# A hybrid decoder step: the chunked mixers' tiles overlapped, and the sample tile's state products on 64 rows, two heads side by side

## What is computed

```python
def _mlstm(...):            # A, by chunks, the carried state is (C, n, m)
    s = einsum('bthd,bjhd->btjh', qc, kc) * exp(d_log - m_t)
    num = einsum('btjh,bjhd->bthd', s, vc) + w_inter * einsum('bthk,bhkv->bthv', qc, C)
    den = sum(s, axis=2) + w_inter * einsum('bthk,bhk->bth', qc, n)
    h = num / maximum(abs(den), exp(-m_t))
    C_new = carry_w * C + einsum('bjh,bjhk,bjhv->bhkv', w_j, kc, vc)
def _retention(...):        # B, the carried state is R
    s = einsum('bthd,bjhd->btjh', qc, kc) * d_mask
    o = einsum('btjh,bjhv->bthv', s, vc) + xi * einsum('bthk,bhkv->bthv', qc, R)
    R_new = g_chunk * R + einsum('jh,bjhk,bjhv->bhkv', zeta, kc, vc)
def _rwkv7(...):            # D, one step per token on S
    s_kk = einsum('bhvk,bhk->bhv', S, kk_t)
    S = S * w_t - s_kk * (kk_t * a_t) + v_t * k_t
    o_t = einsum('bhvk,bhk->bhv', S, r_t)
```

## Time and profile before

| | |
|---|---|
| median of three timed runs | 2622.53 us (2621.73 to 2622.9) |
| the profiled execution | 2619.64 us |
| its span, first to last instruction | 2617.4 us |
| mean granted clock of TensorE | 0.956 |

### The profile page before, as it was taken

How to read it: one execution, slowest core, us unless ns; L and a number is a source line. 1 busy time by engine, 2 the same in 40 slices (tenths; PEclk the granted TensorE clock), 3 DMA queues, 4 the chain that set the end, 5 groups by cost and what they waited for, 6 DMA issues and landing times. The chain is left out here.

```text
span 2617.4 us, 31827 instructions
## 1 busy us (share of the span) xinstructions
PE 2467.3 (94%) x13578; PEld 1809.7 (69%) x13578; DVE 813.1 (31%) x1619; ACT 465.1 (18%) x983; POOL 110.6 (4%) x208
## 2 busy tenths in 40 slices
PE   7989998888999999999989899988799999999997
PEld 6867674463784788888877667654548748888886
DVE  4242233534032644000132422434340336430012
ACT  2332122001130222100023321120111312220000
POOL 0011100000000000000001111000000000000000
PEclk9999988969999999999999999889699999999999
DMA  7101002222442222222131011022233432222220
GB/s 259 65 33 35 33 1 86 67 85 99 161 157 101 81 97 72 89 65 65 65 115 65 33 34 34 33 90 61 84 123 121 164 121 72 77 84 65 83 78 35
DMA packets 137675, 215.07 MB, mean 82 GB/s; under 512 B 35528, under 2 KB 69632, under 8 KB 137408
## 3 DMA queue, kind: packets, MB, share of 16 engines
q1 hardware_dynamic: 135232, 208.84, 23.5%
q10 hardware_dynamic: 2304, 4.20, 0.4%
HBM read 198.43 MB, written 14.58 MB: 81 GB/s over the span
## 5 line engine op out<-in xcount | busy, mean ns | idle before, releaser
L2118 PE MATMUL psum<-big,ring 128*128 128x288 f32 (+1 forms) x2048 | 471.2, 393 | 0.0
L2118 PEld LDWEIGHTS psum<-big,ring 128*128 128x128 f32 x2048 | 388.5, 190 | 79.9 <-DMA ring<-in_w_down 0.4
L580 PE MATMUL psum<-xT,ring 128*128 128x256 f32 (+1 forms) x1536 | 360.6, 397 | 8.6 <-DMA ring<-in_w_in 6.0
L580 PEld LDWEIGHTS psum<-xT,ring 128*128 128x128 f32 x1536 | 294.0, 192 | 70.8 <-DMA ring<-in_w_in 6.3
L627 PE MATMUL psum<-xT,ring 128*128 128x256 f32 (+1 forms) x768 | 227.1, 423 | 0.2
L2061 PE MATMUL psum<-tmp 128*128 128x272 f32 x768 | 181.4, 393 | 0.0
L2061 PEld LDWEIGHTS psum<-tmp 128*128 128x128 f32 x768 | 145.8, 190 | 30.8 <-issue 0.8
L627 PEld LDWEIGHTS psum<-xT,ring 128*128 128x128 f32 x768 | 136.8, 195 | 43.0 <-issue 15.3
L331 DVE SCALAR_TENSOR_TENSOR xtok<-xtok,psum 128x256 f32<-128x256 f32 (+1 forms) x40 | 16.3, 407 | 442.4 <-PE psum L2052 421.3
L624 PE MATMUL psum<-ring,ext 128*128 128x512 f32 x256 | 128.2, 640 | 4.3 <-ACT ext L1581 4.3
L2393 PE MATMUL psum<-ring,big 128*128 128x512 f32 x256 | 113.1, 595 | 0.0
(11 more groups left out here) (437 smaller groups left out, 2783.6 us busy)
## 6 DMA issues: line engine op xcount, KB each, us to landing
ring<-in_w_down SPq DMA_DIRECT2D x16, 2048.0 KB, 8.0
ring<-in_w_in SPq DMA_DIRECT2D x14, 2048.0 KB, 8.4
ring<-in_w_up SPq DMA_DIRECT2D x14, 2048.0 KB, 8.4
big<-in_cache_mem_k SPq DMA_DIRECT2D x16, 1024.0 KB, 5.4
ring<-in_xa_wk SPq DMA_DIRECT2D x4, 2048.0 KB, 8.0
ring<-in_xa_wv SPq DMA_DIRECT2D x4, 2048.0 KB, 9.8
ring<-in_w_out SPq DMA_DIRECT2D x4, 2048.0 KB, 8.8
tmp<-in_cache_mem_v SPq DMA_DIRECT2D x8, 1024.0 KB, 10.2
```

The costliest lines, as they stand in the source:

```text
L580: ins = pe.matmul(ps[:m, :w], lhsT_list[k], rhs(k)[:, c], start=(k == 0), stop=(k == n - 1))
L2118: ins = pe.matmul(ps, w[r][:, k, i * P:(i + 1) * P], hT[:, 2 * KC * r + k, c], start=(r == 0 and k == 0), stop=(r == 1 and k == 2 * KC - 1))
```

## The change

Four things.

1. Every state product of the sample tile takes only the 64 rows of its own head, and the loop over the two heads `a` is inside that over the sequences, so that products of rows 0-63 and rows 64-127 alternate. D's output products move ahead: they stand behind the key products, accumulate into a bank that a product with zeros has cleared, and the other terms are added later. Those of A and B stand ahead of their tile's other products. A's denominator from n takes one product of the block sum `sum64` with `qn`, the query times n, instead of 64 rows with `n0x`.
2. PE's loop over the tiles of A and B is shifted: behind B's outputs of tile T come the transposes, gates and A's scores of tile T+1 (`front`), then spare products, B's scores of T+1, then A's outputs of T.
3. VectorE normalises tile T-1 and updates A's state within its loop for T, behind the weights of T. `Wm`, `kw`, `vt` of A exist twice.
4. The units of spare work are 10 once, then 10 and 8 a tile, instead of 10, 6 and 4.

```diff
-            Wm = cols(xtok, 4288, H, P)
-            kw = cols(tmp, dbase, 2, P)
-            vt = cols(tmp, dbase + 256, 2, P)
+            Wm_a = [cols(xtok, 4288, H, P), cols(xtok, 2560, H, P)]
+            kw_a = [cols(tmp, dbase, 2, P), cols(xtok, 2048, 2, P)]
+            vt_a = [cols(tmp, dbase + 256, 2, P), cols(xtok, 2304, 2, P)]
...
-            n0x = cols(big, 28 * NT + 1024, 2, NB, HD)
+            qn = cols(tmp, dbase + 2992, 2, NS)
...
-            FILL_AB = (10, 6, 4)
+            FILL_AB = (10, 10, 8)
...
                             ps = bk.begin(pe, ("KS",), 2)[:, 0:64].rearrange("p (q t) -> p q t", q=2)
                             for pr in range(2):
-                                for a in range(2):
-                                    for b in range(NB):
-                                        ins = pe.matmul(ps[a * HD:a * HD + HD, pr, TS * b:TS * b + TS], SsT[:, pr, b, :],
-                                                        dpad[:, pr, a, 0, TS * b:TS * b + TS], start=True, stop=True)
+                                for b in range(NB):
+                                    for a in range(2):
+                                        r = slice(a * HD, a * HD + HD)
+                                        ins = pe.matmul(ps[r, pr, TS * b:TS * b + TS], SsT[r, pr, b, :],
+                                                        dpad[r, pr, a, 0, TS * b:TS * b + TS], start=True, stop=True)
                             bk.filled(ins, ("KS",))
+                            out_s = bk.begin(pe, ("os",), 3)[:, 0:64].rearrange("p (q t) -> p q t", q=2)
+                            pe.matmul(out_s, ident, const("drop_a")[:, 0:64], start=True, stop=False, skip_group_check=True)
+                            for pr in range(2):
+                                for b in range(NB):
+                                    for a in range(2):
+                                        r = slice(a * HD, a * HD + HD)
+                                        ins = pe.matmul(out_s[r, pr, TS * b:TS * b + TS], SsT[r, pr, b, :],
+                                                        dpad[r, pr, a, 1, TS * b:TS * b + TS],
+                                                        start=False, stop=False, skip_group_check=True)
+                            sig.up(ins, "Dstates")
                             swap(0)
                             spare_products(pe, ("KS",), FILL_4, (0, 1))
                             bk.given(pe, ("KS",))
-                            ps = bk.begin(pe, ("KSt",), 3)[:, 0:256].rearrange("p (q v) -> p q v", q=2)
+                            ps = bk.begin(pe, ("KSt",), 7)[:, 0:256].rearrange("p (q v) -> p q v", q=2)
...
-                            ps = bk.begin(pe, ("os",), 3)[:, 0:64].rearrange("p (q t) -> p q t", q=2)
+                            pe.wait_ge(sig["Dstates"], sig.at("Dstates", 1))
                             for pr in range(2):
                                 for a in range(2):
-                                    o = ps[a * HD:a * HD + HD, pr, :]
+                                    o = out_s[a * HD:a * HD + HD, pr, :]
                                     pe.matmul(o, Dtok[:NS, 3, pr, a * HD:a * HD + HD], KM[:NS, 2 * pr + a, 1, :NS],
-                                              start=True, stop=False, skip_group_check=True)
-                                    pe.matmul(o, SAn[:NS, 2 * pr + a, :], BM[:NS, 2 * pr + a, 1, :NS],
                                               start=False, stop=False, skip_group_check=True)
-                                    for b in range(NB):
-                                        ins = pe.matmul(o[:, TS * b:TS * b + TS], SsT[:, pr, b, :],
-                                                        dpad[:, pr, a, 1, TS * b:TS * b + TS],
-                                                        start=False, stop=(b == NB - 1), skip_group_check=True)
+                                    ins = pe.matmul(o, SAn[:NS, 2 * pr + a, :], BM[:NS, 2 * pr + a, 1, :NS],
+                                                    start=False, stop=True, skip_group_check=True)
                             bk.filled(ins, ("os",))
...
-                        w_, k_, v_ = (Wm, kw, vt) if pre == "A" else (Wm_b, kw_b, vt_b)
+                        w_, k_, v_ = (Wm_a[T % 2], kw_a[T % 2], vt_a[T % 2]) if pre == "A" else (Wm_b, kw_b, vt_b)
                         q_, x_ = (qspad, vx2) if pre == "A" else (qspad_b, vx2_b)
+                        if T == 4:
+                            pe.wait_ge(sig[pre + "s"], sig.at(pre + "s", 16 * 2))
+                            pe.wait_ge(sig[pre + "qs"], sig.at(pre + "qs", 1 if pre == "A" else 2))
+                        both_ = bk.begin(pe, (pre + "nd", T), bank)
+                        nd = both_.rearrange("p (w q t) -> p w q t", w=2, q=2)
+                        if T == 4:
+                            for w in range(2 if pre == "A" else 1):
+                                pe.matmul(nd[:, w, :, :n], ident, const("drop_a")[:, 0:2 * n], start=True, stop=False, skip_group_check=True)
+                            for pr in range(2):
+                                for b in range(NB):
+                                    for a in range(2):
+                                        r = slice(a * HD, a * HD + HD)
+                                        ins = pe.matmul(nd[r, 0, pr, TS * b:TS * b + TS], (Cs if pre == "A" else Rs)[r, pr, b, :],
+                                                        q_[r, pr, a, TS * b:TS * b + TS], start=False, stop=False, skip_group_check=True)
+                            if pre == "A":
+                                ins = pe.matmul(nd[:, 1, :, :n], const("sum64"), qn, start=False, stop=False, skip_group_check=True)
+                            sig.up(ins, pre + "states")
                         bk.given(pe, (pre + "sc", T))
                         bk.given(pe, (pre + "tr", T))
                         if T:
...
                             pe.wait_ge(sig["Azero"], sig.at("Azero", 1))
                         if pre == "B" and T < 4:
                             pe.wait_ge(sig["Bqx"], sig.at("Bqx", T + 1))
-                        if T == 4 and pre == "A":
-                            pe.wait_ge(sig["n0x"], sig.at("n0x", 1))
                         if T == 4:
-                            pe.wait_ge(sig[pre + "s"], sig.at(pre + "s", 16 * 2))
-                            pe.wait_ge(sig[pre + "qs"], sig.at(pre + "qs", 1 if pre == "A" else 2))
-                        both_ = bk.begin(pe, (pre + "nd", T), bank)
-                        nd = both_.rearrange("p (w q t) -> p w q t", w=2, q=2)
+                            pe.wait_ge(sig[pre + "states"], sig.at(pre + "states", 1))
                         for w in range(2 if pre == "A" else 1):
                             for pr in range(2):
                                 o = nd[:, w, pr, :n]
                                 for a in range(2):
                                     left = (v_[:n, pr, a * HD:a * HD + HD], const("ones")[:n, :])[w]
-                                    pe.matmul(o[a * HD:a * HD + HD, :], left, w_[:n, 2 * pr + a, :n],
-                                              start=True, stop=False, skip_group_check=True)
+                                    ins = pe.matmul(o[a * HD:a * HD + HD, :], left, w_[:n, 2 * pr + a, :n],
+                                                    start=(T < 4), stop=(T == 4), skip_group_check=True)
                                 if T < 4:
                                     state = ((Cb, nb_)[w] if pre == "A" else Rb)[:, pr, :]
                                     right = X2[:, pr, t0:t0 + n] if pre == "A" else qx[:, pr, :]
                                     ins = pe.matmul(o, state, right, start=False, stop=True, skip_group_check=True)
-                                else:
-                                    for a in range(2):
-                                        for b in range(NB):
-                                            state = (Cs if pre == "A" else Rs)[:, pr, b, :]
-                                            if w:
-                                                state = n0x[:, pr, b, :]
-                                            ins = pe.matmul(o[a * HD:a * HD + HD, TS * b:TS * b + TS], state,
-                                                            q_[:, pr, a, TS * b:TS * b + TS],
-                                                            start=False, stop=(b == NB - 1), skip_group_check=True)
...
-                    for T in range(5):
+                    def front(T):
                         keys_values("A", T, 4)
                         gate_tiles(T)
                         key_scores("A", T, 7)
                         keys_values("B", T, 5)
-                        key_scores("B", T, 6)
-                        spare_products(pe, ("ab", T, 0), FILL_AB[0], (3, 3))
+                    front(0)
+                    key_scores("B", 0, 6)
```

(28 more changed lines are left out.)

## The result

The changed kernel takes 2537.67 us (median of four runs, 2533.99 to 2544.39) beside 2622.13 for the kernel before (four runs, 2613.55 to 2622.9). The ratio is 0.9685, with a 95% interval of 0.9665 to 0.9705. The forecast was 2546 with a range of 2530 to 2571: 84.5 us were gained and 76.4 had been worked out. "Rows" are rows of the trace, two to an fp32 product, unless rows of the array are named.

The account below looks back on a forecast made before the run. TensorE, busy 94% of the span, was taken to bound the kernel. Terms of -8.0, -18.2 and -12.0 gave -38.2 us a layer, -76.4 in all: 2543, or 2546 us as the timed median, range 2530 to 2571.

Parts of the forecast that it names:

- Part 1: RWKV (D's) sample tile: narrow alternating state products and earlier outputs save 8.0 us a layer.
- +0.8: D's key and output products together make PE 1.6 us later at swap 0; about half returns: +0.8 a layer.
- Outputs' old place: Where D's outputs stood, 7.24 us, only eight intra products stay, 1.4 us: -5.8 a layer.
- the -3.0: D's swap 3 and four spare units run at the high clock level, 2.84 us instead of 5.85.
- Part 2: Tiles 0 to 3 of A and B: three periods of 18.7 us, 56.1 against 74.3, save 18.2 a layer.
- Rival 2: In every tile a new PE wait of some 3 us for VectorE replaces the removed one: 2564 us, chance 0.14.
- Part 3: From tile 3's outputs to the end of the sample tile, 50.0 us before: -12.0 us a layer.
- -2.7 and +2.7: Last stretch: waits of 2.36 and 0.37 us lie under tile 3's spare work (-2.7); spare rows moved there cost +2.7.
- B's -4.0: Last stretch: B's 64 state rows, at 3.17 us per 32, become 2.05 us plus 0.2 of clearing: -4.0.
- rival 5: More than the sum: A's products at the high level (-1.8 a layer), shorter slow stretches around norms (-3): 2536 us, chance 0.10.
- rival 3: Slower: the clock stays low in the whole stage because narrow products and short waits are denser: 2654 us, chance 0.02.
- rival 1: The two heads' state products do not overlap, by the skill's bank rule: +11.3 us a layer, 2569 us, chance 0.08.

Follow-up runs that it names:

- kernel with the overlap alone: The changed kernel with all state products as before (128 rows, head by head, D's outputs at their old place), leaving only the tile overlap: 2574.09 us, ratio 0.9817.
- kernel with the sample tile alone: The kernel before with only the sample tile of mixers A and B changed (narrow alternating state products, block-sum normaliser): 2595.98 us, ratio 0.9898.
- The repeat: The changed kernel once more, unaltered, timed beside the other runs on the same chip: 2539.70 us, ratio 0.9688.

## Why the prediction was right

**Part 1, D's sample tile: -8.0 forecast, -10.1 and -7.0 measured.** The steps, for layer 0 and then layer 1. Key and output products with what follows up to the transposes (L919 before, L935 after): 9.39 us before, 8.88 and 11.98 after, so -0.5 and +2.6 where I had +0.8. I took the second group at 0.056 a row and half of it returned later; layer 0 has it at 0.032, layer 1 at 0.056, and there nothing returned: the swap and spare rows behind it take 5.82 us, for 5.10 before. Outputs' old place: 7.24 to 0.60, -6.6 and not -5.8. This term was mis-sized: I left the eight terms that stay at 0.35 a pair, 1.4 in all, and they take 0.6. They now stand directly behind each other, with the heads' columns changing every two products; that this is why they are cheaper is likely but no run has it alone. The swap and spare rows: 5.85 to 3.00, -2.85 for -3.0. So the size of the -3.0 was right and its reason was not: the kernel with the outputs back has a stage of 39.94 us, the mean of the changed kernel's two layers, so the place is worth nothing. There the swap and spare rows take 4.45 us, so half of the -2.85 comes with the shorter products; the other half comes with the place, and is paid behind the key products, where the changed kernel's layers take 8.88 and 11.98 us and that kernel 6.59. The sum came out because errors in it cancel, and with -10.1 and -7.0 neither layer has the -8.0. The 3.57 us of waiting stayed, as said.

**Part 2, the tiles: -18.2 forecast, -18.3 measured.** Here every term was read from a row at the high level, and it came out so: 18.70, 18.63 and 18.69 a period, with one wait of 0.7 to 0.8. VectorE's busy time is 31.9 us in three tiles for 34.6 before, and its 5 us of normalising and state end 10 us early. Rival 2, a new wait in each tile, did not happen.

**Part 3, the last stretch: -12.0 forecast, -11.9 and -13.0 measured.** Term by term for layer 0: to B's state products 15.45 to 14.86, -0.6, where I had -2.7 and +2.7. B's products 6.92 (543.68 to 550.60) to 2.87, -4.05 for -4.0. The outer products, 4.56 to 5.21, +0.65; I had nothing. A's products 16.49 to 8.55, -7.9 for -8.0. The tail is 6.68 both times. But the reason given for B's -4.0 was only partly right. I priced the change from 128 rows at 3.17 per 32 to narrow ones at 0.032, and the 3.17 is a price at the low level. The kernel with the overlap alone shows 4.0 us for B's products and all that goes with them, still wide and head by head: the wait's removal, behind which the clock is high, gives 2.9 of the 4.05, and the pairs then 1.1. The kernel with the sample tile alone has the pairs and keeps the wait: 4.14 us (541.43 to 545.57), so there the pairs give 2.8 and the wait's removal would give 1.3. Either gives most of it by itself; that is part of why the parts do not add up. The sum of this part is right in some measure by luck: B's -4.0 needed both changes, and the -0.6 in front and the +0.65 of the outer products cancel. A's products were at the low level, 3.58 for 64, as taken. VectorE was not late: B's first outer products follow at once, and the wait before the next ones is 0.67 where it was 0.86.

**The rest.** 6.8 us of the first profile's gain lie in untouched stretches. The repeat has them only at the end of the span, 2.7 us; the rest varies from execution to execution. Without them the forecast would have missed by 2 us, with them by 8. The median of 2537.67 is nearer to rival 5 (2536) than to the forecast, but rival 5's reasons did not come: A's products ran at the low level (3.58 us for 64 rows), and the stretch with the norms, from the long wait to tile 0's outputs, stayed at 42.7 us. No state load was waited for, rival 2's wait did not appear, and the clock of the tiles was 1.00, so that nothing of rival 3 is there.

**The rule.** The cited rule on row tiles and banks made rival 1, 2569 us. The rows of L917, L926 and L1066 fall under it and run at 0.032 at the high level, so the trace decides against it here. What rival 1 would have cost, 22.6 us by my sum, is 19.9 in the kernel without alternation.

## What to carry to other kernels

Small products that write to different halves of the columns should be written in turn: two then ran in the time of one, on 64 and on 128 rows of the array alike, so here the loop order was worth all of it and the narrower operands nothing. A wait costs its own time and, in this kernel, about half as much again (14.7 us of waits gone gave 22.4, 9.5 gave 14.9), since the work behind it runs at the low clock level; so first place work that is needed anyway under waits, and count what was moved in the trace, because units may be rounded. A step with no cost in one schedule may have one in another: two copies of 0.7 us each cost 1.6 to 2.5 a layer where PE waited for VectorE, and nothing where it did not. And parts that each shorten the same wait or the same slow spell do not add up, even if their medians seem to.

## What the runs showed of the hardware

- 64x4 and 128x4 products of two column halves in turn: 64 rows in 2.03 and 2.08 us at the high level, 3.58 both at the low one. From start to start this is a pair every 58 and every 107 ns; head by head it is mostly one row every 58 and every 107 ns.
- Lengths of one stretch fall on few values some 1.5 us apart, the same in many kernels: 38.4, 39.9 and 41.5 for D's sample tile, 42.7 and 44.2 for the stretch behind it. The longer value has the lower mean clock: 0.96, 0.91 and 0.88 over D's sample tile, 0.84 and 0.81 behind it. What sets the value that a layer takes was not tried.
- Eight 512-column rows moved to where the clock was low took 6.67 us in one layer and 5.37 in the other, where they take 3.60 at the high level. Moving them there gained nothing.
